# Dilated attention's first pair of heads one ring unit later in a hybrid decoder trunk

## What is computed

```python
def reference(x, ...):
    for l in range(DEPTH):                                # 2 layers
        h = _rmsnorm(x, ln_g[l])
        u = h @ w_in[l]
        ...
        y_c = _mla(...) * silu(g_c)                       # 4 heads
        dq = _rope(_rmsnorm(d_q, dil_q_g[l]), positions)  # 4 heads of 128
        dk = _rope(_rmsnorm(d_k, dil_k_g[l]), positions)
        y_d = _dilated_attention(dq, dk, d_v) * silu(g_d)
        x = x + concat([y_a, y_b, y_c, y_d]) @ w_out[l]

def _dilated_attention(q, k, v):
    for w, d in ((128, 1), (512, 4), (2048, 16)):         # keys t, t-d, t-2d, ... down to t-w
        scores.append(q . k[taps] * 128 ** -0.5)
    p = softmax(concat(scores))
    return sum(p_c @ v[taps_c])
```

## Time and profile before

| | |
|---|---|
| median of 3 runs | 807.24 us (807.17 to 807.83) |
| the profiled execution | 806.72 us, its span 804.9 us |
| busy: PE, PE weight load | 99%, 84% |
| busy: DVE, ACT, POOL | 76%, 58%, 16% |
| granted TensorE clock | 9 tenths or more of full speed in all 40 slices |
| HBM traffic | 221 GB/s over the span |

### The profile page before, as it was taken

One profiled execution on the slowest core, in us unless ns is written; L12 is line 12 of the kernel. 1 busy time (PEld: TensorE's weight loads), 2 busy tenths in 40 slices (PEclk: granted clock), 3 DMA queues, 4 the chain that ended last, 5 costly groups with the idle time before them and its releaser, 6 DMA issues.

```text
span 804.9 us, 10724 instructions
## 1 busy us (share of the span) xinstructions
PE 796.2 (99%) x3900; PEld 674.0 (84%) x3900; DVE 608.1 (76%) x1066; ACT 469.2 (58%) x762; POOL 127.5 (16%) x199
## 2 busy tenths in 40 slices
PE   8999999999999999999999999999999999999998
PEld 5888888999887888888888888889998888888886
DVE  6678889787899776665764967988779987865552
ACT  6666543857955676443556465447777566664431
POOL 7100000020432421102100000002105242211000
PEclk9999999999999999999999999999999999999999
DMA  8966534575698987869866655365767988968563
GB/s 332 344 219 215 182 132 152 160 252 187 211 283 262 288 256 243 261 208 280 259 213 187 194 152 196 111 188 170 228 200 238 268 277 256 274 196 286 187 195 115
DMA packets 54117, 178.22 MB, mean 221 GB/s; under 512 B 7408, under 2 KB 8352, under 8 KB 54064
## 3 DMA queue, kind: packets, MB, share of 16 engines
q1 hardware_dynamic: 44736, 149.98, 57.2%
q0 software_dynamic: 9008, 27.34, 12.3%
q10 hardware_dynamic: 320, 0.21, 0.1%
HBM read 161.76 MB, written 15.75 MB: 221 GB/s over the span
## 4 chain that ended last, share of the span: by engine, by line
PE 78%; DVE 12%; issue 3%; ACT 3%; DMA 3%; POOL 0%; SPq 0%; DVEq 0%; ACTq 0%; POOLq 0%
PE gemm L764 24%; PE gemm L755 24%; PE gemm L756 23%; DVE w_lo L1434 4%; DVE arena L1395 3%; DMA raw<-in_weights_dram 1%; DMA arena<-dil_q_squares 1%; PE pairs L921 1%; ACT w_hi L1051 1%; DVE u L1694 1%; PE pairs L811 1%; DVE arena L1523 1%; ACT arena L1231 1%; DMA mla_P_squares<-u 1%; PE pairs L946 0%
## 5 line engine op out<-in xcount | busy, mean ns | idle before, releaser
L1434 DVE TENSOR_TENSOR w_lo<-raw,w_hi 128x1024 fp32r<-128x1024 f32 (+2 forms) x279 | 322.1, 1163 | 151.8 <-ACT w_hi L1051 150.7
L755 PE MATMUL gemm<-w_hi,a_hi 128*128 128x512 f32 (+2 forms) x1080 | 414.5, 384 | 0.7 <-ACT w_hi L1051 0.7
L756 PE MATMUL gemm<-w_hi,a_lo 128*128 128x512 f32 (+2 forms) x1080 | 408.9, 379 | 0.0
L1051 ACT ACTIVATE w_hi<-raw 128x1024 fp32r<-128x1024 f32 (+2 forms) x279 | 278.2, 1011 | 212.7 <-PE gemm L764 138.6
L764 PE MATMUL gemm<-w_lo,a_hi 128*128 128x512 f32 (+2 forms) x1080 | 278.2, 379 | 0.3
L755 PEld LDWEIGHTS gemm<-w_hi,a_hi 128*128 128x128 f32 x1080 | 202.9, 188 | 37.3 <-issue 1.7
L756 PEld LDWEIGHTS gemm<-w_hi,a_lo 128*128 128x128 f32 x1080 | 202.9, 188 | 33.5
L764 PEld LDWEIGHTS gemm<-w_lo,a_hi 128*128 128x128 f32 x1080 | 199.5, 188 | 36.4 <-DVE w_lo L1434 1.9
L637 POOL TENSOR_TENSOR st<-st,powers 128x4 f32<-128x4 f32 (+2 forms) x8 | 3.7, 461 | 296.6 <-ACT arena L1129 213.0
L1081 ACT ACTIVATE u<-gemm,st 128x512 f32<-128x512 f32 (+2 forms) x36 | 21.3, 644 | 14.6 <-PE gemm L764 14.6
L1395 DVE STREAM_TRANSPOSE arena<-u 32x256 f32<-32x256 f32 x64 | 27.9, 436 | 1.2
(11 more groups left out here) (218 smaller groups left out, 672.8 us busy)
## 6 DMA issues: line engine op xcount, KB each, us to landing
raw<-in_weights_dram SPq DMA_DIRECT2D x225, 512.0 KB, 4.3
raw<-in_weights_dram SPq DMA_DIRECT2D x38, 384.0 KB, 3.6
raw<-in_weights_dram SPq DMA_DIRECT2D x16, 344.0 KB, 3.3
y_squares<-arena POOLq DMA_DIRECT2D x8, 512.0 KB, 3.4
arena<-y_squares POOLq DMA_DIRECT2D x32, 128.0 KB, 5.5
x<-in_x_dram SPq DMA_DIRECT2D x4, 512.0 KB, 6.2
o<-ssd_rows SPq DMA_DIRECT2D x8, 256.0 KB, 5.3
param_rows<-in_params_dram SPq DMA_DIRECT2D x2, 904.0 KB, 6.6
```

The source lines that it names most:

```text
L755: pe.matmul(acc_t[t], a_hi[:, k, tok[t]], hi, start=k == 0, stop=False)
L756: pe.matmul(acc_t[t], a_lo[:, k, tok[t]], hi, start=False, stop=False)
L1051: A_(w_hi[:, g % SPLIT, 0:c], raw[:, g % RAW, 0:c], ACT.Copy).then_inc(hi_done, 1)
L1434: TT(w_lo[:, g % SPLIT, 0:c], raw[:, g % RAW, 0:c], w_hi[:, g % SPLIT, 0:c].bitcast(F32), ALU.subtract).then_inc(split_done, 1)
```

## The change

Three entries of `PE_AT` grow by one: `dil S 0` from 99 to 100, `dil PT 0` from 102 to 103, `dil O 0` from 104 to 105. PE's own order of jobs stays. On ACT, `mla PT 1` now stands before `dil P 0`, and `dil PT 0` behind `evac 11`. On DVE, the maxima and taps of the first pair come behind `w_lo` of slot 103 where they came behind that of slot 102, and `dil O 0` comes behind `y 2` and its squares. POOL's and SP's streams are as they were. No instruction is added or removed.

```diff
-          "mla S 1": 94, "mla O 0": 98, "dil S 0": 99, "mla O 1": 102,
-          "dil PT 0": 102, "dil S 1": 103, "dil O 0": 104, "dil PT 1": 106, "dil O 1": 108}
+          "mla S 1": 94, "mla O 0": 98, "dil S 0": 100, "mla O 1": 102,
+          "dil PT 0": 103, "dil S 1": 103, "dil O 0": 105, "dil PT 1": 106, "dil O 1": 108}
...
     "act":
-        "mla rT, mla P 0, ssd rs sum, mla P 1, evac 10, mla PT 0, dil q, dil P 0, mla PT 1, dil PT 0, "
-        "evac 11, dil P 1, dil PT 1, yT 0, yT 1, yT 2, evac 12, yT 3",
+        "mla P 0, ssd rs sum, mla P 1, evac 10, mla PT 0, dil q, mla PT 1, dil P 0, evac 11, dil PT 0, dil P 1, dil PT 1, yT 0, "
+        "yT 1, yT 2, evac 12, yT 3",
...
     "dve":
-        "dil max 0, dil nmax 0, dil P 0, mla ri 1, mla O 1, dil max 1, dil nmax 1, dil P 1, dil ri 0, dil O 0, y 2, y 2 squares, yT 0, dil ri 1, dil O 1, yT 1, "
+        "y 1 squares, y 0, y 0 squares, mla ri 0, mla O 0, dil max 0, dil nmax 0, dil P 0, mla ri 1, mla O 1, dil max 1, "
+        "dil nmax 1, dil P 1, y 2, y 2 squares, dil ri 0, dil O 0, yT 0, dil ri 1, dil O 1, yT 1, yT 2, y 3, y 3 squares, yT 3, "
```

More of the change, by code:

```diff
@@ L253 @@
     "act":
[L254 to L257, removed]
[3 rows of a table removed]
-    "dve":
[L262 to L268, removed]
[3 rows of a table removed]
@@ new lines @@
+        "x rs sum, evac 0, evac 1, gla lr, gla abs, gla exp, gla ln, evac 2, gla E 0, gla E 1, gla E 2, gla cross, gla E 3, "
+        "gla E 4, evac 3, gla E 5, gla E 6, gla E 7, evac 4, ssd abs, ssd exp, ssd eA, ssd ln, conv 3 1, gla rs sum, conv 3 0, "
+        "evac 5, ssd silu 1, mla crs sum, ssd gcol, ssd silu 0, evac 6, ssd exp 0, mla cT, ssd xD, ssd exp 1, mla q 0, evac 7, "
+        "mla q 1, mla rs 0 sum, mla kv 0, mla kv 1, mla rs 1 sum, dil rs 0 sum, evac 8, dil rs 1 sum, mla qT, evac 9, mla rT, "
@@ new lines @@
+        "mla P 0, ssd rs sum, mla P 1, evac 10, mla PT 0, dil q, mla PT 1, dil P 0, evac 11, dil PT 0, dil P 1, dil PT 1, yT 0, "
+        "yT 1, yT 2, evac 12, yT 3",
+    "dve":
+        "pad, gla turn, gla dots, gla zero 0, gla zero 1, gla la, gla scan 0, gla scan 1, gla D 0, gla D 1, gla W 0, gla D 2, "
+        "gla W 1, gla D 3, gla W 2, gla merge 1, gla D 4, gla W 3, gla merge 2, gla D 5, gla W 4, gla merge 3, gla D 6, gla W 5, "
+        "gla merge 4, gla D 7, gla W 6, gla merge 5, gla W 7, gla merge 6, ssd turn, gla merge 7, ssd dt0, ssd dt, ssd la, "
+        "conv 1 0, conv 1 1, gla o, conv 1 2, conv 1 3, conv 1 4, conv 1 5, ssd row, conv 0 0, conv 0 1, conv 0 2, conv 0 3, "
+        "conv 0 4, conv 0 5, ssd CB, mla cn, ssd x squares, ssd E 0, mla cT, ssd E 1, ssd M 0, ssd xdt, ssd M 1, mla n 0 0, "
+        "mla n 0 1, ssd yT, mla q squares, mla n 1 0, ssd y squares, mla n 1 1, mla rope products, mla rope, mla k squares, "
+        "dil n 0 0, dil n 0 1, dil n 1 0, dil n 1 1, dil rope 0 products, dil rope 0, dil rope 1 products, dil rope 1, gated 1, "
+        "mla max 0, mla nmax 0, dil q squares, dil k squares, mla P 0 squares, mla max 1, mla nmax 1, y 1, mla P 1 squares, "
[3 rows of a table added]
```

## The result

| | median | runs | ratio to the kernel before, 95% interval |
|---|---|---|---|
| kernel before | 807.25 us | 6 | |
| changed kernel | 811.65 us | 6 | 1.0051 (1.0031 to 1.0071) |
| changed kernel again (e5) | 810.66 us | 12 | 1.0030 (1.0014 to 1.0046) |
| changed kernel again (e9) | 811.20 us | 9 | 1.0040 (1.0022 to 1.0058) |
| changed kernel again (e14) | 811.16 us | 6 | 1.0058 (1.0040 to 1.0075) |

The change makes the kernel slower by 0.42%, 3.4 us (the four ratios weighted by their runs). I had forecast 808.5 us, 1.3 us slower, with 810.2 as the upper end. The sign was right; the time lies outside the range. The changed kernel's own 33 runs spread from 807.1 to 814.6 us.

The account below looks back on a forecast made before the run. PE, busy throughout its 804.9 us span, was taken as the bound. Later second scores and restarts lose 0.61 + 0.57 + 2 x 0.07 = 1.32 us; 807.24 + 1.3 = 808.5 us, range 806.4 to 810.2.

Parts of the forecast that it names:

- The old stalls go: PE's waits at `dil S 0` vanish, worth 0.77 us in the first layer and 1.06 in the second, 1.83 in all.
- A new wait at `dil S 1`: PE's second dilated scores start 7.24 us after ACT starts `mla PT 1`, 0.61 and 0.57 us later than before.
- The stall at `mla O 1` of 0.2 us at most: PE's wait there for ACT's copy `mla PT 1`, lying inside the wait at `dil S 1`, so costed at nothing.
- the landing at 284.1 and 681.2: When the DMA brings `mla PT 1`'s probabilities in the first and second layer, in us, taken as unchanged.
- The cost that no row has: Slot 107's weight load, some 4 us sooner, beside `mla PT 1`'s probabilities: nothing to 2.6 us, taken near the lower end.
- the first rival: The new wait is also fed by DMA competition from the earlier load: 809 to 811.1 us, chance 0.27.
- the chain: From ACT's `mla PT 1` over `dil P 0` and DVE to PE's `dil S 1`: 7.24 us, a loss of 1.32 us.
- Edits costed at nothing: `dil PT 0` behind `evac 11` on ACT, a later `dil P 1`, and DVE's `dil O 0` at slot 108: no cost.

Follow-up runs that it names:

- e5: Changed kernel run again unchanged, 12 runs: 810.66 us, ratio 1.0030 to the kernel before.
- e9: Changed kernel run a third time unchanged, 9 runs: 811.20 us, ratio 1.0040 to the kernel before.
- e14: Changed kernel run a fourth time unchanged, 6 runs: 811.16 us, ratio 1.0058 to the kernel before.
- e1: Changed kernel with ACT's copy `mla PT 1` reading the first MLA pair's squares, so no wait for the landing (wrong values): 805.15 us, ratio 0.9974.
- e4: Kernel before, run again unchanged for a second trace: 807.16 us, ratio 0.9990 to the kernel before.
- e6: Kernel before with only the weight load of slot 107 released early (first dilated pair's maxima, exponentials, taps at slot 103): 808.70 us, ratio 1.0011.
- e11: Kernel before with `mla PT 1` fed from the first pair's squares, so no wait for the landing (wrong values): 806.33 us, ratio 0.9983.
- e3: Changed kernel with SP holding the weight load of slot 107 until DVE has done the first dilated pair's taps: 809.50 us, ratio 1.0018.
- e8: Changed kernel with POOL sending out the second MLA pair's squares before bringing back `dil k`: 808.74 us, ratio 1.0009 to the kernel before.
- e10: Changed kernel with PE's `dil S 0` alone back at slot 99, DVE and ACT order as changed: 810.37 us, ratio 1.0037 to the kernel before.
- e12: The kernel of e3 run again (changed kernel, load of slot 107 held until the taps): 809.25 us, ratio 1.0021 to the kernel before.
- e15: The kernel of e3 run a third time (changed kernel, load of slot 107 held until the taps): 809.09 us, ratio 1.0020 to the kernel before.
- e2: Changed kernel with the first dilated pair's maxima, exponentials and taps back at slot 102, ahead of `mla PT 1`: 807.28 us, ratio 0.9996 to the kernel before.
- e13: Changed kernel with PE filling its wait before `mla O 1` by unit-matrix matmuls (12 in code, 24 in trace): 812.98 us, ratio 1.0096 to the kernel before.

## Why the prediction was right in its mechanism and wrong in its size

**The old stalls go: right.** No wait at `dil S 0` in any trace of the changed kernel. From `mla O 0` to `mla O 1` PE took 14.35 and 14.61 us in the kernel before and 13.57 in e1's first layer, so the removal is worth 0.78 and 1.04 us, as predicted (0.77 and 1.06). Timeline of PE, the first row of both jobs, the kernel before (with 285.97 and 683.07 of the earlier trace rows) and then e1:

```profile
271.62 0.39 PE L946 MATMUL pairs<-u,arena 128*128 128x128 f32 x2
...
668.46 0.38 PE L946 MATMUL pairs<-u,arena 128*128 128x128 f32 x2
```

```profile
271.52 0.39 PE L946 MATMUL pairs<-u,arena 128*128 128x128 f32 x2
...
285.09 0.39 PE L946 MATMUL pairs<-u,arena 128*128 128x128 f32 x2
```

But that too is one execution's: the stalls were 0.53 and 0.82 us there, 0.77 and 0.17 in e4, 0.71 and 0.40 in e6, and none is listed in e11. Over the runs, e1 is 2.4 us under the kernel before beside it (807.52), which includes what that kernel pays for the landing. e1's ratio is 0.09% under e11's, 0.7 us, which is what the removal was worth where neither waits for the landing; the intervals are too wide to tell it from the predicted 1.83.

**A new wait at `dil S 1`, through `mla PT 1`, `dil P 0`, the taps, two `w_lo` and `mla O 1`: right.** 7.12 to 7.14 us where `dil S 1` waited, in seventeen layers of e3, e5, e8, e9, e10, e12, e14, e15 and the first trace, 7.24 predicted. The hand-over from DVE was 0.14 (from 692.90 + 1.13 to 694.17) and not 0.20; the rest of the difference is hundredths in the other terms. With the early load held the loss is 1.6 us, against a forecast of 1.32.

**The stall at `mla O 1` of 0.2 us at most: wrong**, because it rests on the landing at 284.1 and 681.2. It was 2.43 and 1.91 us in the first profiled execution, 1.53 and 0.92 in e9's, 0.44 and none listed in e5's.

**"The cost that no row has": this is the step that failed.** I bounded the weight load of slot 107 by nothing and by 2.6 us over both layers and took the lower end, "because the loads in front are as long as the landing in question". It measures 1.1 us per layer on the way back, 2.2 in all, and 1.8 us in the time. 1.6 + 1.8 = 3.4 us, which is the loss. So the first rival was the right case, and its 811.1 us the better number, in part by luck: it has 2.6 us for the load, more than was measured, and 1.32 for the chain, less than was measured. The range was cut off inside it: 810.2 leaves out 0.9 of its 2.1 us, which is more than the third that the prediction says. The low value leaned on the Trainium skill's page "DMA: Bandwidth & Descriptors" (queues, rings and completion order), which states that each DMA engine goes round the queue rows it has work for, packet by packet. That one more load in SP's row therefore costs POOL's row nothing was my inference from it, and the mean of the traces disagrees with that. Whether the load took a share on engines whose earlier loads were done, or slowed them all, no run here shows.

**The landing read from one execution: the second fault.** I took one trace's 284.1 as the landing. It varies: the whole way out and back took 13.3 to 17.7 us in the traces without the early load. The kernel before had 0.8 us to spare at `mla O 1`; the change takes 0.77 and 1.06 us away, which is about all of it, and hangs a second consumer on the same event. e2 shows what that costs even without the rest: 1.8 us of gain on paper, none in the median.

**The clock, not foreseen.** In the first trace it took 1.6 us of PE's time, and by the chain only some 0.2 us of that moved `dil S 1`. Over all runs the mean granted clock is 0.9984 against 0.9994 in the kernel before, and 0.9997 with the load held: 0.1% of the span, 0.8 us more of missing clock than before. That is more than it can have cost if, as in the first trace, most of it falls where PE would have waited for DVE. It goes away with the held load, so what it costs is a part of the 1.8 us rather than a term beside it. That reading is argued, not shown; e13 doesn't show it.

**Edits costed at nothing: right as far as can be measured.** e1 shows no cost of `evac 11` or of DVE's later `dil O 0`, and no trace a wait at `dil O 0`.

## What to carry to other kernels

Before a job is moved because its input is late, look at what the same move does to the other engines' order: here it put an exponential, a tap count and two weight splits behind a DMA, and the stall that it removed was smaller than the one it made. When an engine's reordering releases a load earlier, price it as a transfer beside the ones already in flight, above all beside one that a critical wait is about to hang on. And where the argument needs a landing time or a stall, read it from several executions: a wait that is barely absent in one trace was 0.34 us in the next of the same kernel, and a stall of 0.53 or 0.82 us was none in another.

## What the runs showed of the hardware that I had not expected

The same DMA of 384 KB out to memory, with the same POOL work issued ahead of it, took between 6.4 and 10.9 us in different executions and layers, and its return in four parts between 6.1 and 8.5 us with no extra load beside it. A 512 KB load behind other loads in SP's queue slowed a POOL transfer that was already under way, by 1.1 us on the mean of 16 against 14. And the granted TensorE clock went to its lower level (0.50) behind one stall of 2.43 us, about 0.8 us after PE had started again; behind one of 2.06 us in e14's first layer the profile shows no fall (1.00 in every microsecond there).
